# Which partitions stay empty when an expert has fewer tokens than slots: a reordered slot table in a mixture-of-experts step

## The reference, cut to what matters

```python
def moe(x2, w_router, b_router, w_gate_up, b_gate_up, w_down, b_down):
    logits = (x2 @ w_router + b_router).astype(jnp.float32)
    top_v, top_i = lax.top_k(logits, TOP_K)
    gates = jax.nn.softmax(top_v, axis=-1)
    ...
    def expert_block(args):
        xe, e = args
        gu = xe @ w_gate_up[e] + b_gate_up[e]
        gate, up = gu[:, :D_FF], gu[:, D_FF:]
        gate = jnp.minimum(gate, SWIGLU_LIMIT)
        up = jnp.clip(up, -SWIGLU_LIMIT, SWIGLU_LIMIT)
        h = gate * jax.nn.sigmoid(SWIGLU_ALPHA * gate) * (up + 1.0)
        return h @ w_down[e] + b_down[e]
    ...
    return jnp.sum(y * gates[..., None].astype(y.dtype), axis=1)
```

## Time and profile before

| | us |
|---|---|
| median of 3 runs | 1308.9 |
| lowest and highest of the runs | 1306.82 and 1308.98 |
| profiled execution, its own time | 1309.82 |
| profiled execution, span of the trace | 1308.0 |

### The profile page before, as it was taken

How to read it: one execution, slowest core, us unless ns; L and a number is a source line. 1 busy time by engine, 2 the same in 40 slices (tenths; PEclk the granted TensorE clock), 3 DMA queues, 4 the chain that set the end, 5 groups by cost and what they waited for, 6 DMA issues and landing times.

```text
span 1308.0 us, 18424 instructions
## 1 busy us (share of the span) xinstructions
PE 1219.6 (93%) x6214; PEld 775.0 (59%) x6217; DVE 795.7 (61%) x1308; ACT 582.8 (45%) x796; POOL 146.8 (11%) x170
## 2 busy tenths in 40 slices
PE   7999999989989898999999999999999999999971
PEld 5888864436564646757474745564747847474620
DVE  3896758638282929939292926383929928374703
ACT  4112242226272727827272625272737726454502
POOL 9100012020000000000000010100000000101011
PEclk9999999979999999999999999999999999999986
DMA  9620168389999999999999999899999999999995
GB/s 323 93 44 2 39 213 348 144 262 398 410 418 409 420 413 419 411 404 420 414 420 416 420 411 409 294 418 417 422 416 420 417 411 420 418 421 411 424 413 191
DMA packets 67240, 457.46 MB, mean 350 GB/s; under 512 B 15504, under 2 KB 19296, under 8 KB 34404
## 3 DMA queue, kind: packets, MB, share of 16 engines
q1 hardware_dynamic: 56356, 435.28, 81.4%
q0 software_dynamic: 10816, 21.30, 6.8%
HBM read 439.73 MB, written 22.97 MB: 354 GB/s over the span
## 4 chain that ended last, share of the span: by engine, by line
PE 40%; DMA 19%; DVE 13%; issue 5%; ACT 2%; DVEq 0%; POOL 0%; SPq 0%; ACTq 0%; POOLq 0%
PE bank L2259 19%; DMA ring_lo<-in_w_gate_up 14%; PE bank L2399 13%; DVE w_lo L2542 10%; DMA ymix<-ffn_in,idx_next 2%; DMA w_out<-in_w_down 2%; PE bank L2410 2%; ACT w_hi L2039 1%; PE bank L2242 1%; PE bank L2249 1%; DVE cmix L2560 1%; PE bank L2349 1%; PE bank L2375 1%; DVE h_lo L2555 1%; PE bank L2419 0%
## 5 line engine op out<-in xcount | busy, mean ns | idle before, releaser
L2542 DVE TENSOR_TENSOR w_lo<-ring_lo,w_hi 128x1024 fp32r<-128x1024 f32 x256 | 299.0, 1219 | 88.8 <-ACT w_hi L2039 87.8
L2039 ACT ACTIVATE w_hi<-ring_lo 128x1024 fp32r<-128x1024 f32 x256 | 256.4, 1053 | 75.6 <-DMA ring_lo<-in_w_gate_up 49.2
L2399 PE MATMUL bank<-ring_lo,x_s 128*64 128x512 f32 x896 | 203.9, 602 | 1.4 <-issue 1.4
L2259 PE MATMUL bank<-w_hi,x_hi 128*128 128x512 f32 x512 | 167.4, 409 | 8.0 <-DVE x_lo L2548 7.7
L2259 PE MATMUL bank<-w_lo,x_hi 128*128 128x512 f32 x512 | 161.1, 396 | 0.0
L2259 PE MATMUL bank<-w_hi,x_lo 128*128 128x512 f32 x512 | 161.0, 396 | 0.0
L2542 DVE TENSOR_TENSOR w_lo<-w_out,w_hi 128x1024 fp32r<-128x1024 f32 x128 | 152.1, 1218 | 7.0 <-ACT w_hi L2039 7.0
L2039 ACT ACTIVATE w_hi<-w_out 128x1024 fp32r<-128x1024 f32 x128 | 132.7, 1054 | 31.0 <-PE bank L2259 30.9
L1934 POOL DMA_INDIRECT token_sums<-ymix,row_cur x32 | 54.2, 1693 | 717.5 <-ACT ymix L2069 667.0
L2399 PEld LDWEIGHTS bank<-ring_lo,x_s 128*64 128x64 f32 x896 | 61.1, 138 | 113.0 <-issue 111.0
L2259 PEld LDWEIGHTS bank<-w_hi,x_hi 128*128 128x128 f32 x512 | 94.8, 194 | 42.6 <-issue 19.0
(11 more groups left out here) (473 smaller groups left out, 1424.8 us busy)
## 6 DMA issues: line engine op xcount, KB each, us to landing
ring_lo<-in_w_gate_up SPq DMA_DIRECT2D x128, 2048.0 KB, 18.9
w_out<-in_w_down SPq DMA_DIRECT2D x128, 1024.0 KB, 20.4
ring_lo<-in_w_in SPq DMA_DIRECT2D x3, 2048.0 KB, 21.8
w_out<-in_w_out SPq DMA_DIRECT2D x2, 2048.0 KB, 9.5
x<-in_x_prompt SPq DMA_DIRECT2D x6, 512.0 KB, 11.6
ring_lo<-in_w_in SPq DMA_DIRECT2D x2, 1024.0 KB, 10.1
token_sums<-x SPq DMA_DIRECT2D x4, 512.0 KB
ffn_in<-hf SPq DMA_DIRECT2D x4, 512.0 KB, 5.7
```

The lines of the kernel that those rows point to most:

```text
L2039: nc.scalar.activation(high(j), raw(j), ACT.Copy).then_inc(s["w_hi"], 1)
L2259: last = nc.tensor.matmul(bank[b + u][:], v[:, k, :], part(j)[:, u, :], start=(j == 16 and first), stop=(k == KD - 1 and part is high and ...
L2399: last = nc.tensor.matmul(bank[2 * half][64 * u:64 * u + 64, :], x_s[:, k % 4, 64 * (k // 4):64 * (k // 4) + 64], gu[:, k, :, half, 256 * ...
L2542: v.tensor_tensor(low(j), raw(j), high(j).bitcast(F32), ALU.subtract).then_inc(s["w_lo"], 1)
```

## The change

Only the order of the slots in the three tables changes. Each half of 64 partitions is seen as 16 groups of four. A round of 16 slots fills one partition in each group of a half: first groups 1 to 7, then 9 to 15, and as the last two groups 0 and 8, which are partitions 0 to 3 and 32 to 35 of that half. For wide positions a round is done in the lower half, then one in the upper half, and then the next partition of each group. For small positions both halves do the same round (they hold the halves of the same rows). For quarters a round has eight groups per 32 partitions, and group 0 is last. Three table-writing instructions become eight (`iota_s` and `iota_h` in three pieces each, `iota_q` in two). Nothing else in the kernel is touched.

```diff
             v.tensor_copy(iota_c[:], iota_i[:])
-            v.tensor_copy(tb["iota_s"][:].rearrange("p (e f b) -> p e f b", e=16, f=2), iota_i[:].rearrange("p (b f e) -> p e f b", e=16, f=2))
-            v.tensor_copy(tb["iota_h"][:].rearrange("p (h a b) -> p h a b", h=2, b=4),
-                          iota_i[:, 0:S_SLOTS].rearrange("p (b a) -> p a b", b=4).unsqueeze(1).to_broadcast([P, 2, S_SLOTS // 4, 4]))
+            spread_s = tb["iota_s"][:].rearrange("p (h g b) -> p h g b", h=2, b=4)
+            spread_h = tb["iota_h"][:].rearrange("p (h g b) -> p h g b", h=2, b=4)
+            for to, turn in ((slice(1, 8), slice(0, 7)), (slice(9, 16), slice(7, 14)), (slice(0, 16, 8), slice(14, 16))):
+                v.tensor_copy(spread_s[:, :, to, :], iota_i[:].rearrange("p (b h g) -> p h g b", h=2, b=4)[:, :, turn, :])
+                fours = iota_i[:, 0:S_SLOTS].rearrange("p (b g) -> p g b", b=4)[:, turn, :]
+                v.tensor_copy(spread_h[:, :, to, :], fours.unsqueeze(1).to_broadcast([P, 2, turn.stop - turn.start, 4]))
...
-            v.tensor_copy(tb["iota_q"][:].rearrange("p (c a b) -> p c a b", c=4, b=4),
-                          iota_i[:, 0:Q_SLOTS].rearrange("p (b a) -> p a b", b=4).unsqueeze(1).to_broadcast([P, 4, Q_SLOTS // 4, 4]))
+            spread_q = tb["iota_q"][:].rearrange("p (c g b) -> p c g b", c=4, b=4)
+            for to, turn in ((slice(1, 8), slice(0, 7)), (slice(0, 1), slice(7, 8))):
+                fours = iota_i[:, 0:Q_SLOTS].rearrange("p (b g) -> p g b", b=4)[:, turn, :]
+                v.tensor_copy(spread_q[:, :, to, :], fours.unsqueeze(1).to_broadcast([P, 4, turn.stop - turn.start, 4]))
```

## The result

| | before | after |
|---|---|---|
| median of 20 runs each, us | 1308.93 | 1311.41 |
| lowest and highest, us | 1305.83, 1311.06 | 1308.83, 1313.14 |
| ratio, 95% interval | | 1.0019 [1.0013, 1.0025] |
| span of the profiled execution, us | 1308.0 | 1310.1 |

The change costs 2.5 us where 1.15 us of gain were forecast; it ends 0.2 us outside the range. Two places carry it.

What follows compares the result with a forecast made beforehand. The slowest DMA engine was taken to bound the expert loop's two long stretches. A gain of 1.5 us and 0.35 us for tables gave -1.15 us, the median going from 1308.9 to 1307.8 us; range 1304.8 to 1311.2.

Steps and rivals of the forecast that it cites:

- What bounds the loop: Expert loop: two DMA-bound stretches with a PE-bound one between; the slowest DMA engine sets the end of the last weights.
- The grouping: Gathers and scatters: partitions 4g to 4g + 3 and 32 more share one DMA engine, giving sixteen sets of eight.
- The price of a row: Expert loop: a row gathered and scattered costs its engine 0.5 us, taken between 0.40 and 0.55.
- The second stretch then ends 3.0 x 0.5 = 1.5 us earlier: Expert loop, positions 17 to 30: the fullest set falls from 58.5 to 55.5 rows, gaining 1.5 us.
- its twin for the first stretch: Expert loop, positions 0 to 16: the fullest set stays at 92.5 rows, so nothing is gained.
- The drain: Last weights: last engine ends 4.4 us after the mean, two late engines answering to 58.5 and 56.0 rows; shorter after.
- Table writing: Router, DVE: three copies become eight, costing 0.35 us uncovered, 0.3 at least and 0.9 at most.
- The gathers: Chain of waits: the two gathers of 14.90 and 15.93 us stay unchanged.
- A: Faster rival: bias rows load the two sets the change empties; -3.9 + 0.35, about 1305.4 us; chance 0.14.
- B: Slower rival: the change loads the last engine, eight neighbouring partitions sharing one; 3.3 us plus 0.35, 1312.6 us; chance 0.09.
- Its other form: Slower rival's variant: engines 7 and 15 are the late ones and get more rows, 5.5 us; chance 0.03 of the 0.09.
- C: Rival: PE's use of the buffers paces the second stretch, only the 0.35 us of tables remain, 1309.3 us; chance 0.15.

Runs made afterwards that it cites:

- e4: Zigzag slot order (up, then down through the groups), tables written in DVE's idle time, against the kernel before: 1302.73 us, -6.1 us, ratio 0.9957.
- e6: Changed order with each round's groups backwards (7 to 1, 15 to 9, then 0 and 8), tables in DVE's idle time, against the kernel before: 1306.00 us, -3.2 us.
- e3: Changed slot order, its eight table copies moved into DVE's idle time, against the kernel before: 1310.32 us, +1.5 us, ratio 1.0009.
- e2: Old slot order, its three table copies moved into DVE's idle time, against the kernel before: 1307.77 us, -1.1 us, ratio 0.9999.
- e12: Old slot order, tables in DVE's idle time, one bias transfer of four issued, against the kernel before: 1302.40 us, -6.5 us, ratio 0.9956.
- e5: Changed order with groups 1 and 9 last instead of 0 and 8, tables in DVE's idle time, against the kernel before: 1307.85 us, -1.4 us.
- e13: Evened order, fewer rows on lower-half groups 0 to 2, tables in DVE's idle time, against the kernel before: 1302.15 us, -6.4 us, ratio 0.9949.
- e14: e13's order with every group moved on by four, lighter sets at groups 4 to 6, against the kernel before: 1304.00 us, -4.5 us, ratio 0.9961.

## Why the prediction was wrong

- **What bounds the loop** was right: the slowest DMA engine. e4 shows it by evening out rows alone, with 5.0 us.
- **The grouping** (partitions g and g + 32 together, not eight neighbours) was right: e4 and e6 have the opposite sign under the other one.
- **The price of a row**, 0.5 us, was about right: 0.37 by e4 if the fullest set is the last, 0.4 to 0.5 by the distances between the engines with bias rows.
- **The step that failed** is "The second stretch then ends 3.0 x 0.5 = 1.5 us earlier", with its twin for the first stretch (92.5 to 92.5, "nothing is gained there"). It takes the set with the most rows for the last engine, as if engines differed in rows alone. They differ in the bias transfers too: three engines carry them, and the change put the most rows on sets 1 and 2, two of the three by the fit above. In place of -1.5 the loop shows 2.5 - 1.4 = +1.1 in the change itself and +1.3 to +2.5 in e3 against e2. With another group first and the same counts there is a gain, e6 is 2.1 us below e2, but this does not bear out the step: e6 also takes sets 0, 1 and 2 from 58.5, 45.5 and 56.0 rows to 42.0, 47.0 and 49.0.
- **The drain** was read one step too far. That 4.4 us and two engines fit 58.5 and 56.0 rows was taken as a check of rows alone; e12 has these rows, but less bias, and is 5.4 us faster than e2. The lag was 5.1 us, as the windows run on into the norm's load, which the prediction does not mention; with it the check gives 0.46 us a row in place of 0.40. The tail that was to shorten is as long after the change.
- **Table writing** was mis-sized: 0.35 forecast, 0.9 at most, 1.3 to 1.4 measured. The starts of copies were the wrong row for the bound. The right one was in the trace of the kernel before: `order_col`, one column, lasts 1.01 us and ends with POOL's instruction.
- **The gathers** stayed much as they were: the first is 1.1 us longer, the second left the chain, where another one (13.40 us) stands.
- **The rivals.** A named the cause, the bias rows, and put it in the wrong place: on the sets of the partitions that they are written to. So it expected the new fullest set to be free of them and the change to gain. What spoke against A, that the second late engine has no bias rows, does not hold: both late engines carry them. B had the sign right, by a grouping that the runs refute. Its other form does not show either: e6 fills the set of group 7 first and is the fastest order with those counts (-3.2 us). The Trainium skill, "DMA: Bandwidth & Descriptors", section "Latency and other measured facts", calls engines 7 and 15 usually slower; no run here shows it. C charged 0.35 us for tables and nothing for the loop.

The Trainium skill has the rule that was missed. "DMA: Bandwidth & Descriptors", section "Why a DMA increments its semaphore by 16 and not by 1", says that a transfer issued from SP uses the largest number of engines, up to sixteen, that divides the leading sizes of both its sides, and the lowest-numbered ones. By it a transfer of three rows lies on engines 0, 1 and 2, whatever partitions it writes. The section "The descriptor swizzle" of that page gives the engines of a transfer to all 128 partitions; by it engines 0, 1 and 2 are those of sets 0, 1 and 2. The runs agree in the three bursts of bias rows at a position and the three 4-byte packets for a transfer, in the order of e3, e5 and e6 (+1.5, -1.4, -3.2), and in the distances between the three engines. No record names the engines, and e13 against e14 leaves it at 1.9 us with overlapping intervals.

On the tables, the Trainium skill, "SBUF — State Buffer", section "SBUF: two separate sides", says that DVE and GpSimd share a pair of ports that one instruction holds to its end while the other engine waits (on DVE's side for instructions in a two-port mode or with two SBUF inputs). The equal ends of the DVE and POOL rows above agree with it; that waiting was not tried by itself.

Still open: why four more bias transfers cost 20 us when taking away three of the first four gains 5 to 8; what else the lone late engine carries, some 2 us in the second stretch; whether 1302 us is the mean engine's work or another limit; why the bias rows from POOL come late.

## What to carry to other kernels

Before rows are moved between DMA engines, list everything that each engine carries, the small transfers of every step above all: a transfer of few rows lies on few engines (one of three rows on three here), and the order that fills these first loses what the counts promise. Where transfers of uneven rows share engines with a stream that never stops, an order that spreads the early slots over all of them is worth trying, as zigzag was here with 0.4%. And small instructions that are added to a full engine are priced by what they then run beside, or put where the engine waits anyway.

## What was not expected of the hardware

- A transfer of 3 KB cost 0.16 us of the whole program (124 of them 20.1 us), though its rows take each of its three engines only 0.05 us. It leaves one or two of sixteen engines behind (7.4 us at the end); how it comes to 20 us is open.
- A DVE instruction on one column of 32 partitions took 1.00 us beside a POOL instruction of 1.16 us and ended with it; the next one, on 32 columns, took 0.17 us.
- Five kernels with different orders and different bias traffic stand at 1302.15 to 1302.73 us.
